# GpSimd, not VectorE, forms the low half of 14 weight pieces a layer in block one's attention stream

## The reference

```python
h = rmsnorm(x, norm_attn)
proj = h @ w_in                       # split into the inputs of four attentions
o_sb = stick_breaking_attention(...)  # 4 heads, no softmax, a cumulative sum of log(1 - beta)
o_mb = moba_attention(...)            # 4 heads, each query keeps whole blocks of keys
o_ns = nsa_attention(...)             # 4 heads, compressed + selected + window branches, gated
o_df = rmsnorm(diff_attention(...))   # 4 heads, difference of two softmaxes
x = x + concat(o_sb, o_mb, o_ns, o_df) @ w_out
h2 = rmsnorm(x, norm_mlp)
x = x + square(relu(h2 @ w_up)) @ w_down
```

## Time and profile before

| | us |
|---|---|
| median of 3 runs | 3227.64 (3226.57 to 3228.21) |
| the profiled execution | 3227.28 |
| its span in the trace | 3225.5 |

### The profile page before, as it was taken

The page is one execution under the profiler, slowest core; times in us unless marked ns, Lnnn a source line. Parts: engine busy times, 40 slices in busy tenths (PEclk is TensorE's granted clock), DMA queues, the critical chain, the costliest instruction groups (busy, mean ns, idle before and its releaser), DMA issues.

```text
span 3225.5 us, 41774 instructions
## 1 busy us (share of the span) xinstructions
PE 3165.7 (98%) x14512; PEld 2523.7 (78%) x14512; DVE 2026.3 (63%) x3158; ACT 773.8 (24%) x1508; POOL 289.7 (9%) x226
## 2 busy tenths in 40 slices
PE   8999999999999999999999999999999999999998
PEld 7766888887668888888887788888888877788887
DVE  6687655676776555654457865445645477764546
ACT  5575100035751000100014430001200034320003
POOL 2100000021001000200012410000000014300001
PEclk9999999999989999999999999999999999999999
DMA  7211322232112222222222222222222222222222
GB/s 254 75 59 59 101 98 97 92 136 93 53 56 98 98 98 94 90 98 98 94 95 92 73 80 96 98 98 88 96 92 99 92 91 90 73 91 98 91 97 72
DMA packets 86879, 301.97 MB, mean 94 GB/s; under 512 B 9387, under 2 KB 10155, under 8 KB 86488
## 3 DMA queue, kind: packets, MB, share of 16 engines
q1 hardware_dynamic: 81300, 287.68, 26.3%
q10 hardware_dynamic: 5444, 12.52, 1.2%
HBM read 298.03 MB, written 6.06 MB: 94 GB/s over the span
## 4 chain that ended last, share of the span: by engine, by line
PE 90%; DVE 4%; issue 2%; ACT 2%; DVEq 2%; DMA 0%; ACTq 0%; POOL 0%; SPq 0%; POOLq 0%
PE acc L625 20%; PE acc L627 20%; PE acc L626 20%; PE acc L1087 2%; PE acc L789 2%; PE acc L1089 2%; PE acc L1088 2%; PE acc L729 2%; PE acc L730 2%; PE acc L728 2%; PE acc L790 2%; PE acc L791 2%; PE outp L1018 1%; PE score L980 1%; PE trans L992 1%
## 5 line engine op out<-in xcount | busy, mean ns | idle before, releaser
L1778 DVE TENSOR_TENSOR wL<-wraw,wH 128x1024 fp32r<-128x1024 f32 x412 | 529.9, 1286 | 31.3 <-issue 0.6
L625 PE MATMUL acc<-opH,wH 128*128 128x512 f32 x1280 | 497.9, 389 | 0.0
L626 PE MATMUL acc<-opL,wH 128*128 128x512 f32 x1280 | 497.9, 389 | 0.0
L627 PE MATMUL acc<-opH,wL 128*128 128x512 f32 x1280 | 497.9, 389 | 0.0
L625 PE MATMUL acc<-hidH,wH 128*128 128x512 f32 x1072 | 417.0, 389 | 0.0
L626 PE MATMUL acc<-hidL,wH 128*128 128x512 f32 x1072 | 417.0, 389 | 0.0
L627 PE MATMUL acc<-hidH,wL 128*128 128x512 f32 x1072 | 417.0, 389 | 0.0
L1773 DVE CAST wH<-wraw 128x1024 fp32r<-128x1024 f32 x412 | 293.9, 713 | 133.9 <-PE acc L627 115.6
L1649 ACT ACTIVATE big<-acc 128x512 f32<-128x512 f32 x84 | 50.4, 601 | 1162.2 <-PE acc L627 1156.0
L626 PEld LDWEIGHTS acc<-opL,wH 128*128 128x128 f32 x1280 | 240.3, 188 | 50.0
L625 PEld LDWEIGHTS acc<-opH,wH 128*128 128x128 f32 x1280 | 240.3, 188 | 49.9
(11 more groups left out here) (379 smaller groups left out, 5055.2 us busy)
## 6 DMA issues: line engine op xcount, KB each, us to landing
wraw<-in_weights SPq DMA_DIRECT2D x507, 512.0 KB, 3.2
wraw<-in_weights SPq DMA_DIRECT2D x32, 384.0 KB, 2.9
big<-bias_scratch ACTq DMA_DIRECT2D x10, 512.0 KB, 3.6
big<-in_par ACTq DMA_DIRECT2D x2, 1536.0 KB, 6.4
bias_scratch<-bias_rows SPq DMA_DIRECT2D x8, 320.0 KB, 7.8
big<-in_x SPq DMA_DIRECT2D x4, 512.0 KB, 7.9
mixT<-bias_scratch ACTq DMA_DIRECT2D x2, 1024.0 KB, 5.1
out_x<-big SPq DMA_DIRECT2D x8, 256.0 KB, 2.2
```

Of the source, the lines that this page charges most:

```text
L625: pe.matmul(accum[:, :], wH[:, slot, w], hi[:, k, :], start=k == 0, stop=False)
L626: pe.matmul(accum[:, :], wH[:, slot, w], lo[:, k, :], start=False, stop=False)
L627: mm = pe.matmul(accum[:, :], wL[:, slot, w], hi[:, k, :], start=False, stop=k == n - 1)
L1778: dve.tensor_tensor(wL[:, slot, :], wraw[:, slot, :], wH[:, slot, :].bitcast(F32), ALU.subtract).then_inc(split_done, 1)
```

## The change

GpSimd makes `wL` for `LOW_BY_POOL`, the calls n = 22 to 35: the ten pieces of `STREAM` and o0 to o3, 14 a layer, 28 in all. VectorE's calls for them go. GpSimd's additions of line 2530, which stood in a plain loop, and the new subtractions are laid out in one loop over the steps: `SEL_STEP` gives the additions of units 0, 1, 2, 3, 8, 9, 10 and 11 at steps -1, 0, 1, 2, 3, 8, 9 and 10, and the subtraction for a piece that ends at step s stands at step s + 1 (the last at step 50), behind an addition of the same step. Each subtraction waits for `high_done`; the first also waits until VectorE's earlier splits are counted. After the loop VectorE waits once, until all 14 are counted, before `add_group(8)` and its own further splits.

```diff
+LOW_BY_POOL = range(A_AT["k2"], R_ATT * SLOTS + OUT_A)
+SEL_STEP = {u: max([v + 1 for v in range(u) if UNITS[v].part == 0], default=0) - 1
+            for u, x in enumerate(UNITS) if x.kind == "nsa" and x.part == 0}
...
-                    for name in STREAM:
-                        if i == PIECE_STEP[name] + 2:
-                            split_for(A_AT[name])
...
-                        if i == step + 2 and closes_piece(y):
-                            split_for(R_ATT * SLOTS + y // NC)
...
-                    if step + 2 >= N_STEPS and closes_piece(y):
-                        split_for(R_ATT * SLOTS + y // NC)
+                dve.wait_ge(split_done, layer * (ROUNDS1 * SLOTS) + (SLOTS + LOW_BY_POOL.stop))
...
-                for u, x in enumerate(UNITS):
-                    if x.kind != "nsa" or x.part == 1:
-                        continue
+                done = layer * (ROUNDS1 * SLOTS)
+
+                def select(u):
+
+                    x = UNITS[u]
...
+                def low_part(n):
+
+                    slot = n % SLOTS
+                    pool.wait_ge(high_done, layer * ((R_ATT + R_OUT) * SLOTS) + (n + 1))
+                    if n == LOW_BY_POOL.start:
+                        pool.wait_ge(split_done, done + (SLOTS + n))
+                    pool.tensor_tensor(wL[:, slot, :], wraw[:, slot, :], wH[:, slot, :].bitcast(F32), ALU.subtract
+                                       ).then_inc(split_done, 1)
+
+                settle(pool, (sel_done, layer + 1))
+                for i in range(-1, N_STEPS):
+                    for u, step in SEL_STEP.items():
+                        if i == step:
+                            select(u)
+                    for name in STREAM:
+                        if i == PIECE_STEP[name] + 1:
+                            low_part(A_AT[name])
+                    for y, step in enumerate(OUT_STEP):
+                        if i == min(step + 1, N_STEPS - 1) and closes_piece(y):
+                            low_part(R_ATT * SLOTS + y // NC)
```

More of the change, by code:

```diff
@@ L2516, in _ @@
                 at = layer * MAPS1
-                settle(pool, (sel_done, layer + 1))
-                for u, x in enumerate(UNITS):
-                    if x.kind != "nsa" or x.part == 1:
-                        continue
+                done = layer * (ROUNDS1 * SLOTS)
+                def select(u):
+                    x = UNITS[u]
                     width = tiles_of(x)
-                    before = max([v for v in range(u) if UNITS[v].part == 0], default=None)
+                    before = max([v for v in SEL_STEP if v < u], default=None)
                     for hh in range(2):
```

## The result

The changed kernel takes 3248.65 us, the median of 6 runs (3245.84 to 3252.76); the kernel before takes 3227.28 (3226.14 to 3228.21) in 6. The ratio is 1.0066, 95% interval 1.0056 to 1.0076: 21.4 us slower, where 10 were forecast and 3248.0 was the upper end of the range. The direction and the mechanism were right; the forecast had about half of the size that came. The measured time is that of the rival "the losses grow" (3248), which had a chance of 0.13.

The account below looks back on a forecast made before the run. TensorE was taken to lead in most of the streams, VectorE's queue in late stick and diff steps. Pieces 4.5 plus tail 0.5 made 5.0 us a layer, 10.0 for two: 3237.6 us, range 3224 to 3248.

Parts of the forecast that it names:

- the losses grow: Rival, both streams: TensorE's clock falls, late unit 10 additions and covered pieces show; 10 to 15 us more, 3248; chance 0.13.
- GpSimd's price of 2.41 us: Each 128x1024 subtraction on GpSimd, estimated from 512- and 256-column rows: 2.41 us, between 2.05 and 2.6.
- k4's term: Subtraction after k4, layer 0: either held or just missed, between -1.1 and +1.3 us; taken as +0.3.
- the prediction's own rule: At each piece, VectorE's two-input or fast one-input SBUF instruction stands until GpSimd's ends; hold less 1.14 us is the cost.
- The relief of 1.14 us: VectorE's queue: each subtraction taken away is worth 1.14 us, 32 us for all 28.
- v4: Subtraction after v4, layer 0: VectorE's second scan ends 2.4 us later; less 1.14, +1.3 us.
- v5, q5, k5 and o0: Subtractions after these pieces, layer 0, where VectorE leads: +1.2, +1.1, +1.0 and -0.4 us.
- The eight costed at nothing: Subtractions after k2, v3, q3, k3, q4, o1, o2, o3: TensorE's work hides both relief and loss; 0 us.
- The cover: Where TensorE leads: its own work hides the 1.14 us saved and the 1 to 1.3 us lost per piece.
- The tail wait: End of each layer's stream: VectorE waits for GpSimd's last subtraction before evacuating; 0.5 us, between 0 and 1.1.
- The order on GpSimd: Unit 10's addition behind v3's subtraction may delay VectorE up to 2.4 us a layer; taken as 0.
- the relief counts: Rival, VectorE-led stretches: GpSimd mostly runs beside instructions it does not hold, held under 1.14 us; 3220 us; chance 0.12.

Follow-up runs that it names:

- the six: Changed kernel, but GpSimd subtracts only after v4, k4, v5, q5, k5 and o0, VectorE the other eight: 3244.2 us, ratio 1.0045 to before.
- the gated kernel: Changed kernel with ten pieces a layer on GpSimd, in halves, each released when VectorE is about to read PSUM scores: 3219.7 us, ratio 0.9972 to before.
- the repeated subtractions: Changed kernel with VectorE subtracting the same 14 pieces a layer again at its old places: 3275.5 us, ratio 1.0146 to before.

## Why the prediction was wrong in size

- **The mechanism was right.** VectorE's instructions stand until GpSimd's ends. GpSimd's price of 2.41 us was measured as 2.35 to 2.41 unhindered; the holds at v5 and q5 were put at 2.3 and 2.2 and were 2.06 and 2.00 (2.22 and 2.17, less the usual 0.16 and 0.17).
- **The step that failed is k4's term.** It was put at +0.3 a layer, as a draw between -1.1 and +1.3. Taking away the hold alone gave 4.9 a layer, 9.7 us in all; set against the kernel before, k4's section in the six's trace is longer by 4.8 us in layer 0 and by 3.3 in layer 1, where before already stood at the lower clock level. So the term was too small by 3 to 4.6 us a layer, 6 to 9 of the 11.1 us by which the whole was undersized. Three things were wrong in it. The draw fell on the bad side, GpSimd at 218.43 and VectorE at 218.50, 0.07 us apart, and 0.05 in layer 1; but by the prediction's own rule that alone makes 2.15 - 1.14 = +1.0. The relief of 1.14 us was set against the hold, though VectorE's subtraction there was hardly what TensorE waited for: without any subtraction on either engine layer 0's section is 20.35 us and not 20.38. And no price was put on TensorE's clock: 2.8 us of the loss lie behind the idle time, at the lower level. The rival "the losses grow" named the clock, but with 3 us in one layer.
- **v4 was low too**: 2.9 us in both layers of the six's trace and not 1.3. The hold itself was 2.15 us; part of the rest is again the clock, 0.93 in that section where before had 1.00.
- **v5, q5, k5 and o0** were put at 2.9 us and grew their two sections by 2.5 in layer 0 of the six's run and by 1.5 in layer 1: about right.
- **The eight costed at nothing** cost 5.5 us in all with the tail, not 1. The cover was there in part: the holds are seen in the sections (+1.4 to the 2nd evacuation in both layers, +1.5 to the 8th), but so is the relief of k3. The tail wait, put at 0.5, was 0.1 us. These parts, k4's and v4's make more than 11.1 us together: the terms do not simply add.
- **The order on GpSimd** was taken as 0; no run contradicts it, but 1 to 3 us could not have been told.
- **The rival "the relief counts"** fell for this placement, but its condition, a held time below 1.14 us, is what the gated kernel brings about (0.2 to 0.33 us a half in the rows above); there the relief does count.

Not settled: why the repeated subtractions cost 27 us, what makes TensorE's clock fall where it does, and how much of the 12.5 us in layer 0 against 7.0 in layer 1 is the clock. Before, layer 1's stream stood at 0.95 and took 2.9 us more than layer 0's at 0.99; after, they stand at 0.95 and 0.96. By these rows some 3 of the 5.5 us between the layers would be the clock that layer 0 lost, an estimate.

## What to carry to other kernels

Where two engines hold each other up, as GpSimd and VectorE do here, moving work to the one relieves the other only if it stands where the other runs instructions that it does not hold. Compare the time held with the time relieved for each instruction, subtract the relief from the hold only where both are on the same chain, and ask what the bottleneck's clock does behind a longer gap. If GpSimd must take elementwise work from VectorE, cut it to the length of VectorE's PSUM reads and release it by VectorE's own semaphore: the same ten pieces a layer cost 7.3 us unplaced and whole, and gained 8.6 placed and in halves.

## What the runs showed of the hardware

- A GpSimd subtraction of 128x1024 float32 takes 2.35 to 2.41 us where nothing delays it, VectorE's 1.22. Beside it VectorE's scans, two-input instructions and fast one-input ones, even on 128x2 numbers, stand for up to 2.2 us; its reads of PSUM (0.56 and 0.55 us beside a half) and the reciprocals (0.166 us at the mean of 80, before and after) run at their usual length. A subtraction of GpSimd that comes up in a scan waits for its end (3.06 us).
- Beside GpSimd's memsets only the fast one-input instructions are held; the scans are not.
- 2.3 us more of idle time on TensorE were followed by matmuls at the lower clock level (0.43 us apart, not 0.23) in both layers, and removing the hold gave 4.9 us a layer back, more than twice its length. The lower level also came at that place behind 0.87 us of idle time, in layer 1 of the kernel before.
